# Attention in a two-layer decoder step: heads as one stream, running sums over a high and a low part

## The reference, cut to what matters

```python
z = jnp.einsum('bqhd,bkhd->bhqk', qb, kb).astype(jnp.float32) * scale + bias
log_1m = jnp.where(mask, jax.nn.log_sigmoid(-z), 0.0)
log_w = jax.nn.log_sigmoid(z) + lax.cumsum(log_1m, axis=3, reverse=True) - log_1m
w = jnp.where(mask, jnp.exp(log_w), 0.0)
outs.append(jnp.einsum('bhqk,bkhd->bqhd', w.astype(vb.dtype), vb))
```

## Time and profile before

| | us |
|---|---|
| three runs, median | 2430.1 |
| the profiled execution, its own time | 2429.5 |
| its span, first to last instruction | 2427.9 |
| TensorE (PE) busy | 2383.0 |
| VectorE (DVE) busy | 1241.0 |
| ScalarE (ACT) busy | 995.2 |
| GpSimd (POOL) busy | 115.2 |

### The profile page before, as it was taken

One profiled execution on the slowest core, in us unless ns is written; L12 is line 12 of the kernel. 1 busy time (PEld: TensorE's weight loads), 2 busy tenths in 40 slices (PEclk: granted clock), 3 DMA queues, 4 the chain that ended last, 5 costly groups with the idle time before them and its releaser, 6 DMA issues.

```text
span 2427.9 us, 43808 instructions
## 1 busy us (share of the span) xinstructions
PE 2383.0 (98%) x18802; PEld 2184.1 (90%) x18802; DVE 1241.0 (51%) x1725; ACT 995.2 (41%) x1399; POOL 115.2 (5%) x232
## 2 busy tenths in 40 slices
PE   6999999999999999999999999999999999999998
PEld 5999999965699999999999999887777999999998
DVE  5533246755576333357523347755554758633245
ACT  5422235635456222346422235533223546522243
POOL 0000000122100000000000000012222100000000
PEclk9999999999999999999999999999999999999999
DMA  8655345773536653565754255645545356632254
GB/s 308 180 183 182 127 147 177 252 233 113 193 114 227 216 169 96 189 203 174 266 179 161 83 167 187 188 156 164 171 165 165 133 177 183 205 129 87 87 179 155
DMA packets 114724, 417.14 MB, mean 172 GB/s; under 512 B 15195, under 2 KB 19419, under 8 KB 114275
## 3 DMA queue, kind: packets, MB, share of 16 engines
q1 hardware_dynamic: 81026, 301.96, 39.0%
q10 hardware_dynamic: 18144, 62.03, 7.1%
q0 software_dynamic: 15360, 50.34, 6.1%
HBM read 390.85 MB, written 23.43 MB: 171 GB/s over the span
## 4 chain that ended last, share of the span: by engine, by line
PE 86%; DVE 5%; ACT 3%; DMA 2%; issue 2%; SPq 1%; POOLq 0%; POOL 0%; ACTq 0%; DVEq 0%
PE PS L2027 70%; PE PS L1426 3%; PE PS L1961 2%; DVE WL L2319 2%; PE PS L1991 1%; PE PS L1356 1%; ACT WH L2141 1%; DMA RAW<-in_w_in 1%; PE PS L1310 1%; PE PS L1341 1%; PE PS L1351 1%; ACT Y L2192 1%; PE PS L1322 1%; PE PS L791 1%; PE PS L1405 1%
## 5 line engine op out<-in xcount | busy, mean ns | idle before, releaser
L2319 DVE TENSOR_TENSOR WL<-RAW,WH 128x1024 fp32r<-128x1024 f32 (+1 forms) x478 | 633.0, 1325 | 647.8 <-ACT WH L2141 647.2
L2027 PE MATMUL PS<-HH,WH 128*128 128x260 f32 x3432 | 796.8, 285 | 3.9 <-DVE QKVS L1120 1.7
L2027 PE MATMUL PS<-HH,WL 128*128 128x260 f32 x3432 | 786.5, 283 | 0.0
L2027 PE MATMUL PS<-HL,WH 128*128 128x260 f32 x3368 | 769.5, 283 | 0.0
L2141 ACT ACTIVATE WH<-RAW 128x1024 fp32r<-128x1024 f32 (+1 forms) x478 | 542.1, 1135 | 423.0 <-PE PS L2027 260.3
L2027 PEld LDWEIGHTS PS<-HH,WH 128*128 128x128 f32 x3432 | 569.9, 188 | 26.5 <-issue 16.8
L2027 PEld LDWEIGHTS PS<-HH,WL 128*128 128x128 f32 x3432 | 569.4, 188 | 0.0
L2027 PEld LDWEIGHTS PS<-HL,WH 128*128 128x128 f32 x3368 | 556.9, 188 | 0.6 <-issue 0.2
L2027 PE MATMUL PS<-GH,WH 128*128 128x260 f32 x1408 | 386.1, 284 | 1.2 <-DVE WL L2319 1.2
L2027 PE MATMUL PS<-GL,WH 128*128 128x260 f32 x1408 | 384.2, 283 | 0.0
L2027 PE MATMUL PS<-GH,WL 128*128 128x260 f32 x1408 | 383.5, 283 | 0.0
(11 more groups left out here) (340 smaller groups left out, 2319.0 us busy)
## 6 DMA issues: line engine op xcount, KB each, us to landing
RAW<-in_w_in SPq DMA_DIRECT2D x236, 512.0 KB, 3.7
RAW<-in_w_out SPq DMA_DIRECT2D x120, 704.0 KB, 4.0
AW<-in_w_ada ACTq DMA_DIRECT2D x114, 512.0 KB, 5.4
RAW<-in_w_odd SPq DMA_DIRECT2D x60, 512.0 KB, 3.7
RAW<-in_w_odout SPq DMA_DIRECT2D x30, 512.0 KB, 3.9
RAW<-in_w_even SPq DMA_DIRECT2D x28, 512.0 KB, 4.3
KV<-in_v_pages POOLq DMA_DIRECT2D x32, 256.0 KB, 4.7
SR<-in_ret_past POOLq DMA_DIRECT2D x32, 256.0 KB, 4.0
```

The lines of the kernel that those rows point to most:

```text
L2027: last = nc.tensor.matmul(ps[:, x, 0:HT], w[:, k * P:(k + 1) * P], src[k0 + k][:, x, :], start=(begin and t == 0), stop=(end and t == 2))
L2319: nc.vector.tensor_tensor(low_, RAW[:, from_:from_ + w], high_.bitcast(F32), ALU.subtract).then_inc(lo_done, 1)
```

## The change

The running sums change their type. S of a head is rounded to F32R by ScalarE (`high_part`, into `SHA` or `SHB` in turn), VectorE subtracts that from S in place (`low_part`, `spl_done`), and each matmul of `sums` becomes two, over the high and the low part, with `TRI` and `ONES` copied to F32R once.

The heads become one stream. TensorE does the scores of head h + 4 after the sums of head h, block by block, and no longer in pairs. S gets a fifth and a sixth place; heads 6 and 7 reuse those of 0 and 2. |z| of heads 0 to 5 is VectorE's, of 6 and 7 ScalarE's. `log_weights` writes to S and not to Z. The scores of head 1 and `sums_past` move into units 26 and 27. `values_past(1)` to `(3)` are cut into four and go between the steps of heads 3, 5 and 7, and GpSimd's loads follow heads 4 and 7 in its order. Four output transfers count on a semaphore of their own (`pool_out`), and VectorE waits for them at head 1's first block, ScalarE at the first high part.

```diff
+        HOME_OF = (0, 1, 2, 3, 4, 5, 0, 2)
+        ZS = [ZQ[h % 4] for h in range(HEADS)]
+        SP = [SQ5[n] for n in HOME_OF]
+        SPL = [SL5[n] for n in HOME_OF]
+        SPH = [at("SHA", [CAUSAL], sph_at, F32R)[:], at("SHB", [CAUSAL], sph_at + causal, F32R)[:]]
...
+            SCORES_AT = {(25, 3): 0, (25, 4): 1, (26, 1): 2, (26, 2): 3, (26, 3): 4, (26, 4): 5}
...
+            def scores(h, j):
+
+                if h >= HEADS:
                     return
-                pe.wait_ge(z_dve, biased_to(t, j))
-                for e in range(2):
-                    score(2 * t + e, j, PS[0][:, e, 0:LEN[j]]).then_inc(z_done, 1)
+                pe.wait_ge(vp_evac, 2) if 4 * h + j < 10 else pe.wait_ge(z_dve, 4 * h + j - 1)
+                score(h, j, PS[0][:, j % 2, 0:LEN[j]]).then_inc(z_done, 1)
 
             def sums(h, i):
                 if i == 0:
-                    pe.wait_ge(sp_done, h + 1)
+                    pe.wait_ge(spl_done, h + 1)
+                if h + i == 0:
+                    pe.wait_ge(const_ok, 3)
                 n = 4 * h + i
                 pe.wait_ge(lw_done, n - 1) if n >= 2 else pe.wait_ge(vp_evac, 4)
-                last = nc.tensor.matmul(PS[1][:, i % 2, 0:LEN[i]], TRI[:], SP[h % 4][:, OFF[i]:OFF[i] + LEN[i]],
-                                        start=True, stop=(i == 3))
-                for j in range(i + 1, 4):
-                    last = nc.tensor.matmul(PS[1][:, i % 2, (j - i) * P:LEN[i]], ONES[:],
-                                            SP[h % 4][:, OFF[j]:OFF[j] + LEN[j]], start=False, stop=(j == 3))
+                for j in range(i, 4):
+                    w = TRIR if j == i else ONESR
+                    for x, part in enumerate((SPH[h % 2], SPL[h])):
+                        last = nc.tensor.matmul(PS[1][:, i % 2, (j - i) * P:LEN[i]], w[:],
+                                                part[:, OFF[j]:OFF[j] + LEN[j]], start=(j == i and x == 0),
+                                                stop=(j == 3 and x == 1))
                 last.then_inc(s_done, 1)
...
+            for j in range(4):
+                scores(2, j)
+            ada_step("start", 0)
+            for p in range(PAGES):
+                values_past(0, p)
+            for j in range(4):
+                scores(3, j)
+            PAST_AT = {3: 1, 5: 2, 7: 3}
+            VALUES_AT = ((), (0,), (1,), (2, 3))
+            for h in range(HEADS):
                 for i in range(4):
-            sums_past()
-            scores_of_one()
-            ada_step("start", 0)
-            for t in range(PAIRS):
-                scores(t + 1, 0)
-                sums(2 * t, 0)
-                scores(t + 1, 1)
-                if t:
-                    values(t - 1)
-                sums(2 * t, 1)
-                scores(t + 1, 2)
-                sums(2 * t, 2)
-                if t == 2:
+                    sums(h, i)
+                    scores(h + 4, i)
+                    if h % 2 == 0 and h:
+                        for n in VALUES_AT[i]:
+                            values(h // 2 - 1, n)
+                    if h in PAST_AT:
+                        values_past(PAST_AT[h], i)
+                if h == 4:
                     gather(0)
-                scores(t + 1, 3)
-                sums(2 * t, 3)
-                if t < 3:
-                    values_past(t)
-                ada_step("head", 2 * t)
-                for i in range(4):
-                    sums(2 * t + 1, i)
-                if t == 3:
-                    values_past(3)
-                ada_step("head", 2 * t + 1)
+                ada_step("head", h)
             gather(1)
-            values(3)
+            for i in range(4):
+                values(3, i)
 
...
+            def high_part(h):
+
+                act.wait_ge(sp_done, h + 1)
+                if h == 0:
+                    act.wait_ge(pool_out, 64)
+                after(act, s_done, 4 * (h - 2) + 4)
+                nc.scalar.activation(SPH[h % 2], SP[h], ACT.Copy).then_inc(sph_done, 1)
...
+                if i == 27:
+                    high_part(0)
+                    table(EXP_SET)
+            value_rows(0)
             decay(1)
+            for tt in (1, 2, 3):
+            high_part(1)
...
-            for t in range(PAIRS):
-                if t:
-                    outputs(t - 1)
-                if t < 3:
-                    decay_of_pair(t + 1)
-                    table(LOG_SET)
-                if t < 3:
-                    for h in (2 * t + 2, 2 * t + 3):
-                        log(h)
-                    table(EXP_SET)
-                for h in (2 * t, 2 * t + 1):
-                    weights(h)
+            decay(2)
+            table(LOG_SET)
+            log(2)
+            table(EXP_SET)
+            for b in (2, 4, 6):
+                high_part(b)
+                if b > 2:
+                    outputs(b // 2 - 2)
+                else:
+                    decay(3)
+                decay(b + 2) if b < 6 else decay(7)
+                table(LOG_SET)
+                log(b + 1)
+                if b < 6:
+                    log(b + 2)
+                table(EXP_SET)
+                weights(b - 2)
+                weights(b - 1)
+                high_part(b + 1)
+                if b == 2:
+                    decay(5)
+            outputs(2)
+            weights(6)
+            weights(7)
             outputs(3)
...
+            def sized(h):
+
+                dve.wait_ge(z_dve, block_of(h, 3))
+                dve.wait_ge(z_masked, block_of(h, 3))
+                nc.vector.scalar_tensor_tensor(SP[h], ZS[h], -1.0, ZS[h], ALU.mult, ALU.max).then_inc(z_abs, 1)
+
+            def low_part(h):
+                dve.wait_ge(sph_done, h + 1)
+                nc.vector.tensor_tensor(SPL[h], SP[h], SPH[h % 2].bitcast(F32), ALU.subtract).then_inc(spl_done, 1)
 
...
+                    sized(0)
+                    dve.wait_ge(pool_out, 64)
+                    first_scored(1, 0)
+                    first_scored(1, 1)
...
-            for t in range(PAIRS):
-                if t == 2:
+            nc.vector.memset(PS[3][:, 1, :], 0.0).then_inc(z_zero, 1)
+            scored(2, 2)
+            scored(2, 3)
+            softplus(1)
+            sized(2)
+            for j in range(4):
+                scored(3, j)
+            for h in range(HEADS):
+                if h == 4:
                     copy_past(0)
-                scored(t + 1, 0)
-                log_weights(2 * t, 0)
-                scored(t + 1, 1)
-                if t:
-                    low(t - 1)
-                log_weights(2 * t, 1)
-                scored(t + 1, 2)
-                scored(t + 1, 3)
-                if t == 2:
+                if h == 5:
                     copy_turned(0)
-                sized(t + 1, 0)
-                log_weights(2 * t, 2)
-                log_weights(2 * t, 3)
-                sized(t + 1, 1)
-                if t == 0:
-                    softplus(1)
-                ada_evac("head", 2 * t)
-                for i in range(2):
-                    log_weights(2 * t + 1, i)
-                if t < 3:
-                    softplus(2 * t + 2)
-                for i in range(2, 4):
-                    log_weights(2 * t + 1, i)
-                if t < 3:
-                    softplus(2 * t + 3)
-                ada_evac("head", 2 * t + 1)
+                if h:
+                    low_part(h)
+                for i in range(4):
+                    log_weights(h, i)
+                    scored(h + 4, i)
+                if h == 0:
+                    softplus(2)
+                    sized(3)
+                    sized(4)
+                if h == 1:
+                    sized(5)
+                if h in (3, 5):
+                    low((h - 3) // 2)
+                if h % 2:
+                    softplus(h + 2)
+                if h in (1, 3):
+                    softplus(h + 3)
+                ada_evac("head", h)
+            low(2)
...
-            for h in range(2):
+            for h in range(HEADS):
                 for j in range(4):
-                    masked(h, j, 4 * h + j + 1)
-            for t in range(PAIRS - 1):
-                for j in range(4):
-                    for e in range(2):
-                        masked(2 * t + 2 + e, j, 10 * t + 8 + 2 * j + e + 1)
-                pool.wait_ge(kv_used, 4 + t + 1)
-                for n in range(2):
-                    pages(v_pages, 2 * t + 2 + n, n)
+                    masked(h, j)
+                if h in (4, 7):
+                    t = h // 3 - 1
+                    pool.wait_ge(kv_used, 4 + t + 1)
+                    for n in range(2):
+                        pages(v_pages, 2 * t + 2 + n, n)
+            pool.wait_ge(kv_used, 7)
+            for n in range(2):
+                pages(v_pages, 6 + n, n)
```

(3 more changed lines are left out.)

283 lines of the change are left out of this document (143 added, 140 removed).

## The result

The changed kernel takes 2469.05 us (median of 4 runs, 2465.34 to 2470.2) against 2430.27 (4 runs, 2430.02 to 2430.8): ratio 1.0157, 95% interval 1.0139 to 1.0174. The forecast was 2446 us in a range of 2434 to 2456. The direction was right, the measured rise is 2.5 times the one forecast, and the range did not hold the time. Of the experiments' kernels two executions, of 3901.92 us in experiment 9 and 3311.36 us in experiment 13, ran at a low clock over their whole length and are left out of every median and interval.

What follows compares the result with a forecast made beforehand. TensorE was taken to bound the stretch of heads. Sums -15.6, scores +8.8, old waits -3.7, gaps +21.1 and clock +5.1 made +15.7 us, so 2446 us, slower by 0.6%, range 2434 to 2456.

Steps and rivals of the forecast that it cites:

- The gaps: TensorE waiting for VectorE's low parts ahead of the heads' sums, and for the pages of values: +21.1 us.
- The page wait: Loads of the value pages into two buffers, not hidden by one head between uses: 1.9 us, bounds 0 to 3.
- The scores: Scores of heads 2 to 7 lose their pairing, each head costing what a pair did: +8.8 us.
- The sums: Running sums of eight heads as two rounded-type matmuls each: 22.7 in place of 38.3 us, -15.6 us.
- the bound from below: Cheap end for a rounded-type matmul of 128 columns in the sums: half the 260-wide step, 0.055 us.
- The clock: TensorE's clock falls behind three gaps of about 5 us, 1.7 us lost each: +5.1 us, bounds 0 and 8.5.
- the other waits: TensorE's 3.7 us idle in the stretch of heads before the change goes: -3.7 us.
- (a): Rival: the clock stays up through the heads' gaps, +10.6 us, 2441 us; chance 0.25.
- (b): Rival: the sums' narrow matmuls pay float32's price, +6.2 more, +21.9, 2452 us; chance 0.11.
- (c): Rival: VectorE keeps up, gaps 5 us in all and no clock lost, -5.5 us, 2425 us; chance 0.07.

Runs made afterwards that it cites:

- experiment 9: The kernel before with one idle stretch, 6.32 us, made by 16 GpSimd operations ahead of the sums of head 1; 2437.49 us.
- experiment 13: The kernel with two-part sums, paired scores and rewritten VectorE and ScalarE orders, plus one idle stretch ahead of the sums of head 1; 2430.85 us.
- experiment 15: The changed kernel with low part first and pages' values one more head apart, plus one idle stretch ahead of the sums of head 1; 2451.48 us.
- experiment 7: The changed kernel with float32 sums, no high and low parts, and the pages' values one more head apart; 2444.32 us.
- experiment 14: The stream with float32 sums, single scores and pages one more head apart, plus one idle stretch ahead of the sums of head 1; 2449.14 us.
- low-part-first kernel: The changed kernel with VectorE doing the low part of head h + 1 right behind the last subtraction of head h; 2451.56 us.
- experiment 8: The kernel before with only the two-part sums of the change, and VectorE's and ScalarE's orders rewritten; 2424.54 us.

## Why the prediction was right in direction and wrong in size

**The gaps**: right. Booked were 5.3, 5.6, 0.5, 4.6, 1.0 and 2.2 us before heads 1 to 6, and 1.9 for the pages; measured 5.21, 4.89, 1.95, 3.89, 0.67, 1.96 and 0.16, in sum 18.7 us for 21.1. VectorE's low part ended each of the six, as its order said. The page wait was right in kind (7.38, 4.76, 5.82 us once the heads ran faster) and absent here.

**The scores**: right, 2.95 us a head at full clock, the price of a pair.

**The sums**: the narrow matmul was taken at 0.119 us and measured 0.055, the bound from below; the changes of type, which the sum did not have, gave that back: 3.38 us a head in place of 2.84, a saving of 11.3 us and not 15.6. By the Trainium skill's 81 ns ("TensorE: Matmul & The Clock Gate", the back-to-back issue gap) the prediction estimated 20.3 us for eight heads; the trace has 27.0, and its steps of 128 columns are below that gap.

**The clock**: the step that failed, "3 x 1.7 = +5.1 us; bounds 0 and 8.5". It measured 25.9 us. The price of one gap came from the kernel's start and is near what a single one costs (2.1 to 2.8 us in the kernel before). What failed was to take that price for every gap of this kernel and multiply it. Here the low clock behind one gap lasts far longer: 14.3 us behind the one stretch in the relative of experiment 15, 18.7 us behind the second gap with the first one filled. The changed kernel's gaps end at 591.66, 609.82, 629.90 and 653.07, and the work between them lasts 13.3, 18.1 and 19.3 us. Each gap comes before or near the time when the clock would be back, and 68 us become one low stretch. That they join in this way is argued from these lengths. What is shown is that filling one of them gives 7 us (the first) or 12 us (the second) back, and all of them 15 in spite of the new page wait. Why the clock stays down so long behind heads 1 to 3 is open.

**The sum again, with the measured terms**: sums -11.3, scores +8.8, the other waits of the stretch and ahead of it from 6.0 to 2.2 us (-3.9, booked -3.7), gaps +18.7, clock +25.9, in all +38.2 for the 38.9 us between the two profiled executions. Two terms were mis-sized in the same direction, the clock by 20.8 us and the sums by 4.3; the gaps, 2.4 us too dear, gave a little back. With the sums' error alone the time would have stayed in the range.

**The rivals**: (a), the clock stays up, had +10.6 us; without the clock's 25.9 us the measured 38.9 are +13.0, and the sums' 4.3 less the gaps' 2.4 are most of the difference. (b), the dear narrow matmul, is ruled out by its 0.055 us. (c), VectorE keeps up, was right that the two-part sums gain then, but not in the stream: with all gaps ahead of sums under 1.6 us the stream still took 2444.5 us. The gain shows where the pairs stay, at 2424.5.

## What to carry to other kernels

A gap on a busy TensorE is priced with the clock behind it, and a price read from one gap elsewhere in the kernel may not hold: here a single gap was followed by 3.4 to 19 us at the low level, depending on the kernel and the place, and 19 us of gaps cost 26 us of clock. As an upper bound, price the whole distance from one gap to the next at half speed. When an operation becomes cheaper through a pass on another engine, place that pass by when its reader asks, ahead of everything that is for later heads; the same sums were worth -5 us with VectorE's and ScalarE's orders rewritten around the passes and +14 us with the passes put in behind the softplus. A reordering that frees one wait should keep what other work shared: pairs on the two halves of the rows cost nothing extra, and buffers with a turn-around of 12.5 us need that much work between two uses.

## What the hardware showed that was not expected

- The granted clock stood at 0.50 for 68 us in which TensorE had work for 54 us, 5.00 of 5 us busy in several slices. The Trainium skill ("TensorE: Matmul & The Clock Gate", HAM oscillation in real kernels) has idle gaps of microseconds throttle the array; the trace agrees (gaps of 5.21 and 4.89 us), and adds that work alone did not end it soon.
- Many short waits need not do what a long one does: 11.3 us idle in waits of up to 1.24 us left the clock at 1.00 over 79 us, while one of 3.80 us brought it down. Between them it varies. Page waits of 2.59 us (experiment 7, at 660.61) and 3.13 us (experiment 14, at 666.03) left it at 1.00; waits of 0.91 and 0.56 us were followed by a low clock in the low-part-first kernel.
- Two executions of the same code differ. Experiment 13's kernel is experiment 8's up to its stretch. The wait of 1.05 us for the last scores of head 0 left the clock at 1.00 in experiment 8 (first row); in experiment 13 (the other two) the clock was low from 578.8 to 582.8:

```profile
580.85 0.49 PE L693 MATMUL PS<-QP,KP 64*128 64x128 f32 x4 [1.05 <-DVE ZD L1114]
...
578.64 0.66 PE L693 MATMUL PS<-QP,KP 64*128 64x128 f32 x4 [1.05 <-DVE ZD L1116]
580.00:581.00 1.00, 1.00 (x4) 0.14 (x2) 1.00 (x2) 0.00 (x0) 0.38 (x2) 0.50 0.00 0
```

- The first matmul after a change from float32 to the rounded type steps by 0.34 us at 512 columns in place of 0.23, and the first float32 matmul behind a narrow one comes after 0.21 us in place of 0.05 or 0.06: 0.1 and 0.15 us each time.
